# PEER sums of all eight heads accumulate in one pair of PSUM banks, and the first tile's final norm moves between heads 8 and 9

## The reference, cut to what matters

```python
h   = layer_norm(ALPHA * x + mix, ln1_g, ln1_b)              # 256 tokens x 1024
q   = (h @ wq).reshape(256, 8 heads, 2, 128)
v1, i1 = top_k(q[:, :, 0] @ k1.T, 16);  v2, i2 = top_k(q[:, :, 1] @ k2.T, 16)
best, eidx = top_k(of the 16 x 16 sums v1 + v2, 16)          # 16 experts for each token and head
gate = softmax(best)
act  = gelu(einsum('td,tkd->tk', h, u[eidx])) * gate         # 128 experts for each token
ffn  = einsum('tk,tkd->td', act, v[eidx])
out  = layer_norm(ALPHA * h + ffn, ln2_g, ln2_b)
```

## Time and profile before

| | |
|---|---|
| median of 3 executions | 837.9 us (836.54, 837.9, 837.97) |
| span of the profiled execution, first to last instruction | 834.0 us |
| TensorE busy, share of the span | 692.9 us, 83% |
| VectorE busy | 576.7 us, 69% |
| GpSimd busy | 289.4 us, 35% |
| ScalarE busy | 259.5 us, 31% |
| bytes moved | 300.88 MB, mean 361 GB/s |

### The profile page before, as it was taken

How to read it: one execution, slowest core, us unless ns; L and a number is a source line. 1 busy time by engine, 2 the same in 40 slices (tenths; PEclk the granted TensorE clock), 3 DMA queues, 4 the chain that set the end, 5 groups by cost and what they waited for, 6 DMA issues and landing times.

```text
span 834.0 us, 8498 instructions
## 1 busy us (share of the span) xinstructions
PE 692.9 (83%) x2239; PEld 363.9 (44%) x2239; DVE 576.7 (69%) x1419; ACT 259.5 (31%) x765; POOL 289.4 (35%) x267
## 2 busy tenths in 40 slices
PE   6999999999999897787859595958696868687676
PEld 3478565686767443332324242323232323233232
DVE  3499664576756487767686859595858686777845
ACT  1123560216141342332332323232323323232322
POOL 0000000125353574534444343626253535254500
PEclk9999999999999999979998898989798989798999
DMA  8994402198989999999999999999999999999992
GB/s 301 392 345 149 155 1 74 63 404 324 421 339 376 422 421 422 422 420 422 422 422 421 422 421 424 422 422 421 421 421 423 422 422 422 422 421 421 422 421 122
DMA packets 54266, 300.88 MB, mean 361 GB/s; under 512 B 5432, under 2 KB 7776, under 8 KB 21472
## 3 DMA queue, kind: packets, MB, share of 16 engines
q0 software_dynamic: 36864, 268.45, 77.8%
q1 hardware_dynamic: 16160, 31.92, 10.6%
q10 hardware_dynamic: 1216, 0.19, 0.1%
HBM read 299.49 MB, written 1.05 MB: 360 GB/s over the span
## 4 chain that ended last, share of the span: by engine, by line
DMA 39%; PE 39%; issue 9%; DVE 5%; POOL 4%; ACT 3%; DVEq 0%; POOLq 0%; SPq 0%; ACTq 0%
DMA arena<-in_expert_uv,expert 37%; PE bank L627 15%; PE bank L606 7%; PE bank L424 7%; POOL arena L396 4%; PE bank L465 3%; PE bank L560 3%; DVE arena L1292 2%; ACT weight L873 1%; DMA arena<-in_w_idx 1%; PE bank L415 1%; PE bank L614 1%; ACT mid L880 1%; PE bank L531 1%; ACT arena L783 0%
## 5 line engine op out<-in xcount | busy, mean ns | idle before, releaser
L627 PE MATMUL bank<-arena,mid 128*128 128x512 f32 x1024 | 476.6, 625 | 121.8 <-ACT mid L880 121.8
L396 POOL DMA_INDIRECT arena<-in_expert_uv,expert x256 | 287.7, 1124 | 501.1 <-PE bank L627 257.4
L1292 DVE SCALAR_TENSOR_TENSOR arena<-x_sb,arena 128x1024 f32<-128x1024 f32 x256 | 305.6, 1224 | 145.2 <-DMA arena<-in_expert_uv,expert 144.5
L627 PEld LDWEIGHTS bank<-arena,mid 128*128 128x128 f32 x1024 | 202.1, 201 | 390.6 <-issue 238.2
L868 ACT ACTIVATE gelu<-dots 128x4 f32<-128x4 f32 (+2 forms) x68 | 14.0, 205 | 335.9 <-DVE arena L1292 328.1
L880 ACT ACTIVATE mid<-ident,weight 128x128 f32<-128x128 f32 x256 | 82.3, 390 | 6.0
L424 PE MATMUL bank<-arena,x_t 128*128 128x512 f32 (+1 forms) x160 | 66.9, 576 | 8.2 <-DMA arena<-in_w_idx 8.2
L606 PE MATMUL bank<-x_t,arena 128*128 128x128 f32 x512 | 58.8, 275 | 1.3 <-ACTq L843 1.3
L606 PEld LDWEIGHTS bank<-x_t,arena 128*128 128x128 f32 x512 | 58.0, 192 | 2.5 <-ACTq L843 1.5
L873 ACT ACTIVATE weight<-gelu,gate 128x1 f32<-128x1 f32 x256 | 55.1, 284 | 3.2
L424 PEld LDWEIGHTS bank<-arena,x_t 128*128 128x128 f32 x160 | 31.0, 197 | 40.4 <-issue 37.2
(11 more groups left out here) (193 smaller groups left out, 426.2 us busy)
## 6 DMA issues: line engine op xcount, KB each, us to landing
arena<-in_w_in SPq DMA_DIRECT2D x6, 2048.0 KB, 14.6
arena<-in_peer_wq SPq DMA_DIRECT2D x4, 2048.0 KB, 8.1
arena<-in_w_out SPq DMA_DIRECT2D x2, 2048.0 KB, 21.8
arena<-in_expert_uv,expert POOLq DMA_INDIRECT x256, 24.3
arena<-in_w_idx SPq DMA_DIRECT2D x2, 608.0 KB, 8.2
x_t<-in_x_columns SPq DMA_DIRECT2D x2, 512.0 KB, 6.4
x_sb<-in_x SPq DMA_DIRECT2D x1, 1024.0 KB, 17.3
ln_gb<-in_ln_g SPq DMA_DIRECT2D x2, 512.0 KB, 10.0
```

The source lines that it names most:

```text
L396: pool.indirect_dma_start(out=arena[:, slot * SLOT:(slot + 1) * SLOT], out_offset=None, in_=expert_uv, in_offset=bass.IndirectOffsetOnAxis ...
L627: last = mm(banks[2 * parity + half][:, :], lhsT=diag[:, j % 8, :], rhs=arena[:, at:at + 512], start=j == 0, stop=j == SLOTS - 1, skip_gro ...
L1292: ins = stt(rows, x_rows[:, bass.ds(tile * D_MODEL, D_MODEL)], 1.0, rows, ALU.mult, ALU.mult, accum_out=dots[:, parity, j:j + 1])
```

## The change

All eight heads of a tile now accumulate in the same two banks, 0 and 1 for tile 0 and 2 and 3 for tile 1. TensorE starts the accumulation with the first slot of the tile's first unit and stops it with the last slot of the tile's last unit. `take_sum`, the zeroed buffer `ffn` and the semaphore `sum_taken` with its waits are gone. The residual of each tile reads the two banks directly, half by half, inside the norm (`add_sum`). Tile 0's residual and norm stand behind unit 8 instead of behind unit 14. For this the loop over units 3 to 14 becomes a loop of two turns (units 3 to 6), units 7 and 8 written out, and a loop of three turns (units 9 to 14), on each engine. On ScalarE the square root of tile 0's norm moves to the same place, and SP's stores of tile 0, which wait for the norm, follow it.

```diff
+    LOOPS = ((EARLY_UNITS, 2), (PEER_HEADS + 1, 3))
+    CROSSING = (PEER_HEADS - 1, PEER_HEADS)
...
-            def sum_slots(u, parity, some=range(SLOTS), last_unit=False):
-
-                if some[0] == 0 and not (isinstance(u, int) and u == 0):
-
-                    pe.wait_ge(sum_taken, u)
+            def sum_slots(u, tile, some=range(SLOTS), first_unit=False, last_unit=False):
+
                 for j in some:
                     pe.wait_ge(diag_ready, u * SLOTS + j + 1)
                     for half in range(2):
                         at = slots_of(u)[j] * SLOT + D_MODEL + half * 512
-                        last = mm(banks[2 * parity + half][:, :], lhsT=diag[:, j % 8, :], rhs=arena[:, at:at + 512],
-                                  start=j == 0, stop=j == SLOTS - 1, skip_group_check=True)
-                        if last_unit and j == SLOTS - 1 and half == 0:
+                        last = mm(banks[2 * tile + half][:, :], lhsT=diag[:, j % 8, :], rhs=arena[:, at:at + 512],
+                                  start=first_unit and j == 0, stop=last_unit and j == SLOTS - 1, skip_group_check=True)
+                        if last_unit and tile and j == SLOTS - 1 and half == 0:
                             last.then_inc(half_summed, 1)
                     last.then_inc(slot_used, 1)
...
-            def take_sum(u, tile, parity):
-
-                dve.wait_ge(slot_used, (u + 1) * SLOTS)
-                for half in range(2):
-                    where = mix[:, bass.ds(tile * D_MODEL + half * 512, 512)]
-                    ins = tt(where, banks[2 * parity + half][:, :], where, ALU.add)
-                ins.then_inc(sum_taken, 1)
-
-            def add_experts(t):
-
-                link(stt(x_sb[:, t, :], x_sb[:, t, :], ALPHA, ffn[:, t, :], ALU.mult, ALU.add))
+            def add_sum(t, half, part):
+
+                dve.wait_ge(*((half_summed, 1) if t and not half else (slot_used, (t + 1) * PEER_HEADS * SLOTS)))
+                link(stt(x_sb[:, t, part], x_sb[:, t, part], ALPHA, banks[2 * t + half][:, :], ALU.mult, ALU.add))
...
                 for g, group in enumerate(slot_groups(last)):
                     dot_slots(u, tile, parity, group)
-                    if g == 0:
-                        take_sum(u - 1, former_tile, 1 - parity)
-                        if not last:
-                            finish_gate(u + 1, 1 - parity)
+                    if g == 0 and not last:
+                        finish_gate(u + 1, 1 - parity)
...
-            nc.vector.memset(ffn[:, 0, :], 0.0).then_inc(sum_taken, 1)
-            dve.wait_ge(sum_taken, 1)
...
             dve.wait_ge(scores_ready, len(score_order) + 1)
-            link(nc.vector.memset(ffn[:, 1, :], 0.0))
-            with dve.Fori(0, LOOP_TURNS) as i:
...
-            add_experts(0)
-            layer_norm(0, TILES, result_ready, lambda half, part: None)
-            dot_unit(UNITS - 1, TILES - 1, 1, TILES - 1, last=True)
...
+            dot_loop(*LOOPS[0], 0)
+            for u in CROSSING:
+                dot_unit(u, u // PEER_HEADS, u % 2)
             dve.wait_ge(ln2_in, 32)
+            layer_norm(0, TILES, result_ready, lambda half, part: add_sum(0, half, part))
+            dot_loop(*LOOPS[1], 1)
+            dot_unit(UNITS - 1, TILES - 1, 1, last=True)
+            layer_norm(TILES - 1, 2 * TILES - 1, result_ready, lambda half, part: add_sum(TILES - 1, half, part))
```

More of the change, by code:

```diff
@@ L103, in build_layer @@
     EARLY_UNITS = len(early) // SLOTS
-    LOOP_TURNS = (UNITS - 1 - EARLY_UNITS) // 2
+    LOOPS = ((EARLY_UNITS, 2), (PEER_HEADS + 1, 3))
+    CROSSING = (PEER_HEADS - 1, PEER_HEADS)
+    assert LOOPS[0][0] + 2 * LOOPS[0][1] == CROSSING[0] and LOOPS[1][0] + 2 * LOOPS[1][1] == UNITS - 1
     turn = [(j + early[-1] + 1) % SLOTS for j in range(SLOTS)]
@@ L157, in build_layer @@
         peer_q_t = view(mix, D_MODEL, 2, 4, P)
-        ffn = view(mix, 0, TILES, D_MODEL)
         big = sb("big", 4096)
@@ L244, in build_layer @@
         dots_ready, gelu_ready, weight_ready, diag_ready = (sem(n) for n in ("dots_ready", "gelu_ready", "weight_ready", "diag_ready"))
-        slot_used, half_summed, sum_taken = sem("slot_used"), sem("half_summed"), sem("sum_taken")
+        slot_used, half_summed = sem("slot_used"), sem("half_summed")
         result_ready, out_stored = sem("result_ready"), sem("out_stored")
@@ L402, in _ @@
                 gather_unit(u, u % 2)
-            with pool.Fori(0, LOOP_TURNS) as i:
-                gather_unit(2 * i + EARLY_UNITS, EARLY_UNITS % 2)
-                gather_unit(2 * i + EARLY_UNITS + 1, 1 - EARLY_UNITS % 2)
+            with pool.Fori(0, LOOPS[0][1]) as i:
+                for n in range(2):
+                    gather_unit(2 * i + LOOPS[0][0] + n, (LOOPS[0][0] + n) % 2)
+            for u in CROSSING:
+                gather_unit(u, u % 2)
+            with pool.Fori(0, LOOPS[1][1]) as i:
+                for n in range(2):
+                    gather_unit(2 * i + LOOPS[1][0] + n, (LOOPS[1][0] + n) % 2)
             gather_unit(UNITS - 1, 1)
@@ L927, in _ @@
                 weigh_unit(u, u % 2)
-            with act.Fori(0, LOOP_TURNS) as i:
-                weigh_unit(2 * i + EARLY_UNITS, EARLY_UNITS % 2)
-                weigh_unit(2 * i + EARLY_UNITS + 1, 1 - EARLY_UNITS % 2)
+            with act.Fori(0, LOOPS[0][1]) as i:
+                for n in range(2):
+                    weigh_unit(2 * i + LOOPS[0][0] + n, (LOOPS[0][0] + n) % 2)
+            for u in CROSSING:
+                weigh_unit(u, u % 2)
             root_of_variance(TILES)
+            with act.Fori(0, LOOPS[1][1]) as i:
+                for n in range(2):
+                    weigh_unit(2 * i + LOOPS[1][0] + n, (LOOPS[1][0] + n) % 2)
             weigh_unit(UNITS - 1, 1, last=True)
@@ L1294, in dot_slots, with dot_unit @@
                 ins.then_inc(dots_ready, 1)
-            def dot_unit(u, tile, parity, former_tile, last=False):
+            def dot_unit(u, tile, parity, last=False):
                 if not last:
@@ L1325, in _, with dot_loop @@
                 before = count[0]
-                dot_unit(u, 0, u % 2, 0)
+                dot_unit(u, 0, u % 2)
                 per_unit = count[0] - before
-            dve.wait_ge(scores_ready, len(score_order) + 1)
-            link(nc.vector.memset(ffn[:, 1, :], 0.0))
-            with dve.Fori(0, LOOP_TURNS) as i:
-                for n in (EARLY_UNITS, EARLY_UNITS + 1):
-                    u = 2 * i + n
-                    count[1] = i * 2 * per_unit
-                    dot_unit(u, u // PEER_HEADS, n % 2, (u - 1) // PEER_HEADS)
-            count[1] = (LOOP_TURNS - 1) * 2 * per_unit
-            dve.wait_ge(ln2_in, 32)
-            add_experts(0)
-            layer_norm(0, TILES, result_ready, lambda half, part: None)
-            dot_unit(UNITS - 1, TILES - 1, 1, TILES - 1, last=True)
-            dve.wait_ge(sum_taken, UNITS)
-            add_experts(TILES - 1)
-            def add_last_sum(half, part):
-                dve.wait_ge(*((slot_used, UNITS * SLOTS) if half else (half_summed, 1)))
-                link(tt(x_sb[:, TILES - 1, part], banks[2 + half][:, :], x_sb[:, TILES - 1, part], ALU.add))
-            layer_norm(TILES - 1, 2 * TILES - 1, result_ready, add_last_sum)
+            def dot_loop(first, turns, tile):
+                base = count[1]
+                with dve.Fori(0, turns) as i:
+                    for n in range(2):
+                        count[1] = base + i * 2 * per_unit
+                        dot_unit(2 * i + first + n, tile, (first + n) % 2)
+                count[1] = base + (turns - 1) * 2 * per_unit
+            dve.wait_ge(scores_ready, len(score_order) + 1)
+            dot_loop(*LOOPS[0], 0)
+            for u in CROSSING:
+                dot_unit(u, u // PEER_HEADS, u % 2)
+            dve.wait_ge(ln2_in, 32)
+            layer_norm(0, TILES, result_ready, lambda half, part: add_sum(0, half, part))
+            dot_loop(*LOOPS[1], 1)
+            dot_unit(UNITS - 1, TILES - 1, 1, last=True)
+            layer_norm(TILES - 1, 2 * TILES - 1, result_ready, lambda half, part: add_sum(TILES - 1, half, part))
 def kernel(**inputs):
```

29 lines of the change are left out of this document (17 added, 12 removed).

## The result

The changed kernel took 840.4 us (median of nine executions, 838.05 to 841.93), the kernel before 837.8 us on the same chip (nine, 835.78 to 837.97). The ratio is 1.0033, with a 95% interval of 1.002 to 1.0046: slower, where I had forecast 836.6 us and no measurable change. The profiled execution spans 838.8 us and took 840.56, so 1.76 us lie outside the span. Every later profile gave 1.7 to 1.8, which makes the profiled execution of before (834.0 of span) one of about 835.8 us, the fastest of its nine, and not one 2.5 to 4.0 us longer than its span.

A forecast was written before the change was run, and what follows sets the result against it. From about 258 us the kernel was taken as a DMA-bound stream of gathers. All terms were 0 except 1.3 us at the end: span 834.0 - 1.3 = 832.7, median 837.9 - 1.3 = 836.6 us, range 835.1 to 838.6.

The forecast's parts named there:

- the rival of the starved stream: Norm between units 8 and 9 delays slot release beyond 28 us; 840.9 us without the gain, 839.6 with; chance 0.08.
- cover holds: Sign: the stretch from 540 to 600 us, around the moved norm, stays at 420 GB/s or more.
- Additions out of the steady units: VectorE, 1.4 us less work for each unit; it only waits longer for rows, gain 0.
- The wait inside units 1 and 2: VectorE's 12.09 and 8.9 us waits for TensorE go; gain 0, at most 0.98 us.
- the cleared buffers: Two buffer clearings on VectorE and TensorE's waits for `sum_taken` go; gain 0.
- the early rival: Around 240 to 250 us VectorE frees GpSimd, or stores get cheaper: about 835.6 us, with both 834.7; chance 0.13.
- The norm between units 8 and 9: VectorE leaves the rows for 15.8 us, catching up by about unit 9's eleventh row; queued gathers cover it, cost 0.
- The two stores: Tile 0's stores, moved from unit 15 to mid-stream: 2.1 us in both places, difference 0, up to 0.9 gain for the range.
- The end: After unit 14, shorter TensorE idle times keep full clock in the last burst, so the last slot starts earlier: gain 1.3 us.
- The clock rival: TensorE's clock still falls at the end, last burst 22.6 us as now: 837.9 us; chance 0.24.
- My chance of slower: Whole kernel above 839.6 us, from a starved stream and a little from the unknown: 0.11.

The follow-up runs named there:

- the second comparison: The changed kernel, unedited, measured again against the kernel before: 838.75 us against 836.7, ratio 1.0021 [1.001, 1.0033].
- before, written out: The kernel before with units 3 to 14 written out one by one on every engine, no loop: 842.2 us, ratio 1.007.
- PSUM sums, PE split: The changed kernel with only TensorE's loop split and tile 0's norm back behind unit 14: 836.41 us, ratio 0.9995; repeated 837.03, 0.9993.
- GpSimd's kernel: The kernel before with only GpSimd's loop over units 3 to 14 split: 837.6 us in a single execution.
- the norm late: The changed kernel with tile 0's norm back between units 14 and 15, split loops and sums in PSUM kept: 838.88 us, ratio 1.0012.
- The runs with the stores last: Tile 0's stores held behind the last gather: PSUM sums with only TensorE split, 833.46 us, repeated 835.2; kernel before, 835.89 us.

## Why the prediction was wrong

**What failed is a term that the sum left out.** I wrote of the new code only as lateness ("a few more from the new code", in the rival of the starved stream), to be covered by the queue of gathers. The sum had the new code at nothing. Its fetches are traffic on the engines that set the bound, and a queue does not cover traffic. A fetch by VectorE costs up to 0.97 us, and the slips beside them now fall in units 4, 7, 9 and 10 (0.65 + 0.98 + 1.0 + 0.97 = 3.6 us), where before they fell in units 4 and 15 (0.44 + 1.03 = 1.5). The 2.1 between them are the 521.69 - 519.62 of the table; 0.2 of it, in unit 4, is no more than chance, since that slip was 0 and 1.00 in two profiles of one kernel. The corrected sum, up to the first bank read, is 2.1 + 0.2 - 1.2 = 1.1 us. The medians say 2.6 and 2.05, and the interval of the second comparison, 0.8 to 2.8 us, holds 1.1; that of the first, 1.7 to 3.9, does not. What the first has beyond it I could not trace to a place.

Why a block of 8 KB in 300 MB shows at all: a row has landed when the last of 16 DMA engines has finished its part, and the trace has the 16 times for each row, as events of its semaphore. Worked out from them, the gap between the first and the last engine to finish the last row of a unit was:

```
changed kernel:      unit 3 1.9   unit 4 2.6   unit 7 3.6   unit 9 4.6   unit 10 5.5   unit 15 5.5 us
before:              unit 3 1.8   unit 4 2.2   unit 14 2.3   unit 15 3.4
before, written out: unit 3 2.4 ... unit 14 8.2   unit 15 8.1
PSUM sums, PE split: unit 3 2.4 ... unit 15 2.3
```

In these kernels the gap grows at each fetch of VectorE that shows as a slip, and then keeps its size to within 0.2 us. The kernel with only VectorE's loop split shows it best. Against a schedule of one row each 2.4835 us, with 0 for the last engine at unit 3's last row, its 16 engines finished:

| row | last engine | the one before it | first engine |
|---|---|---|---|
| 8.15 | 1.67 | 0.73 | -1.68 |
| 9.15 | 2.66 | 0.76 | -1.67 |
| 10.15 | 3.67 | 0.80 | -1.64 |

One engine falls back by 1.0 us at each step, the other fifteen keep their time. So VectorE's fetches take the same engine each time, as far as the order of finishing can tell, since the trace does not name the engines. A fetch costs the stream only what it pushes its engine behind the last one. In unit 4 that is between 0 and 1.00 us, depending on how far ahead this engine still was; once it is the last itself, each fetch costs all of its 0.97. In GpSimd's kernel it started 1.6 us ahead of the last, so its fetch cost nothing in unit 4 and 0.37 in unit 15. GpSimd's own two fetches pushed an engine that was 2.8 us ahead of the last to 1.6 ahead of it. TensorE's fetches, blocks of 16 KB in q8, each push an engine back by about 1.5 us, but another one each time, and so nearly always one that is still ahead. The exception is the kernel with all loops split: there its slip of 0.96 in unit 4 is one of TensorE's, on an engine that was 0.60 ahead of the last. So it is not VectorE's code as such that costs, but a fetch that falls on an engine which is already last.

The q14 fetch itself is in the changed kernel's queues from 475 to 485 us, in the stretch of the first 0.98 above:

```profile
DMA packets 576, 4.20 MB, mean 420 GB/s; under 512 B 63, under 2 KB 63, under 8 KB 63
## 3 DMA queue, kind: packets, MB, share of 16 engines
q0 software_dynamic: 575, 4.19, 101.1%
q14 instruction: 1, 0.01, 0.2%
```

In the kernel of before the same stretch holds no fetch:

```profile
q0 software_dynamic: 579, 4.22, 101.4%
```

The loss is 4 gather packets of 579. A mean of 420 GB/s where 422 was usual is all that the windows show of it, and I had set 420 as the mark of "cover holds".

The Trainium skill (Runtime: NRT & Kernel Launch, "Instruction fetch mechanics") says that crossing a block boundary is mostly hidden, since the sequencer fetches ahead by its own queue, and that kernels prefer full unrolling. For the engine that fetches, the rows agree: in the changed kernel's stream no VectorE instruction stood idle without a row, a semaphore or another instruction to explain it. For a stream that fills the DMA engines they do not: the written-out kernel took 0.7% longer, and 4.2 of the 6.4 us that its profile took beyond that of before between first gather and first bank are slips.

**Additions out of the steady units, gain 0:** right; 144.5 us of waiting became 176.0. **The wait inside units 1 and 2, gain 0 and at most 0.98; the cleared buffers, 0:** right, the stretch up to unit 2's last row took 138.65 us instead of 138.44. That is also the end of the early rival.

**The norm between units 8 and 9, cost 0:** right in its mechanism. VectorE left its rows at 546.51, the dots resumed at 562.30, 15.8 us as worked out, and it waited for a row again at 9.10, the eleventh, as worked out. The DMA engines stayed full. The starved rival did not occur. With the norm late, the fetch alone gives a slip of 1.00 us at this place; the other 1.2 of the 2.21 are the stores, which moved here with the norm.

**The two stores, 2.1 us in both places:** mis-sized. By bytes I had 1.2; the row at 798.22 made me take 2.1. The other 1.03 was a fetch of VectorE at 795.2. The runs with the stores last show it: in the kernel before with its stores last, that row's slip of 0.98 stays (797.09 to 800.55, with a fetch at 798.45), and the 1.12 of unit 15 goes:

```profile
797.09 1.23 DVE L1293 SCALAR_TENSOR_TENSOR arena<-x_sb,arena 128x1024 f32<-128x1024 f32 x1 [0.85 <-DMA arena<-in_expert_uv,expert]
...
800.55 1.22 DVE L1293 SCALAR_TENSOR_TENSOR arena<-x_sb,arena 128x1024 f32<-128x1024 f32 x1 [2.23 <-DMA arena<-in_expert_uv,expert]
```
The difference of 0 between the places was right, and so was the lower bound.

**The end, 1.3 us:** right. Last dot to bank 3.45 us instead of 4.67, a gain of 1.22; the last slot started at 829.06, 0.45 behind its diagonal's start at 828.61. The clock rival did not occur, but it was nearer than I put it. In other kernels of this study the last burst took longer after idle times of 3.16, 3.39 and 3.40 us (22.40, 23.85 and 23.93 us for 48 records). The 3.48 on which I leaned is no safe bound, as the written-out kernel shows:

```profile
808.25 23.93 PE L626 MATMUL bank<-arena,mid 128*128 128x512 f32 x48 [3.40 <-ACT mid L878]
```

**The numbers.** My chance of slower, 0.11, stood on starvation and a little for the unknown. A range that reached 838.6 counted nothing for the start's spread of 4 us between executions, which no three times could have shown, and nothing for code size, which the static counts and the fetch lines on the page did show.

## What to carry to other kernels

When DMA engines are full, count everything that moves bytes, also what no instruction of the kernel issues: the fetch lines of the page, and the static length of each engine's code before and after. A split loop that only moves work to another place can cost more than the work it hides, while transfers that nobody waits for, such as an early tile's stores, can be worth holding back until the stream has ended: 1.1 to 1.2 us of it here. Compare two profiles from a common event inside the kernel, not from the start, since the start alone differed by 4 us here.

## What the runs showed of the hardware

- A fetch in q14 is 8 KB and in q8 16 KB. In q14 the block takes 0.31 to 0.34 us, and the gather packet right behind it 0.97 instead of 0.31 when the fetch is VectorE's and 0.65 to 0.69 when it is ScalarE's or GpSimd's. TensorE's fetches are those in q8: about 1.0 to 1.1 us, and the packet behind it 0.77 to 0.86.
- 16 engines at 422 GB/s together do not share a gather's load among themselves: one that is behind stays behind, by 8.1 us at the end of the written-out kernel.
- TensorE's granted clock from 100 to 120 us was 1.00, 0.91 or 0.83 in 14 profiles of like mixer code, and 0.91 and 0.83 in two of the same kernel. The first gather was issued between 162.36 and 166.46 us.
- The low clock after an idle time has no fixed length of idle ahead of it here: 3.47 us idle were followed by 7.13 us for 16 records in one kernel, 3.48 by 9.83 in another, both at unit 15:

```profile
794.90 7.13 PE L628 MATMUL bank<-arena,mid 128*128 128x512 f32 x16 [3.47 <-ACT mid L886]
```

```profile
795.89 9.83 PE L627 MATMUL bank<-arena,mid 128*128 128x512 f32 x16 [3.48 <-ACT mid L885]
```
